# Dense stages with token blocks of 364 columns, three to a group, for 272 columns, four to a group

## What is computed

```python
def _rmsnorm(x, g):
    inv = lax.rsqrt(jnp.mean(jnp.square(x), axis=-1, keepdims=True) + RMS_EPS)
    return (x * inv) * g

proj = _rmsnorm(x, g) @ w                       # 1024 -> 3072: q, k, v of two head groups
...
mixed = jnp.concatenate([_rmsnorm(flat(o_a), g_sb), _rmsnorm(flat(o_b), g_dil)], axis=-1) @ w_out
x = x + mixed                                   # 1024 -> 1024
hdn = jax.nn.relu(_rmsnorm(x, g_mlp) @ w_up)    # 1024 -> 4096
return x + jnp.square(hdn) @ w_down             # 4096 -> 1024
```

## Time and profile before

| | us |
|---|---|
| median of 3 runs (2284.97 to 2289.49) | 2288.51 |
| the profiled execution, its own time | 2293.12 |
| its span, first to last instruction | 2291.3 |
| matmuls of TensorE busy in it | 1918.0 (84%) |
| weight loads of TensorE | 1700.2 (74%) |
| VectorE | 894.1 (39%) |
| ScalarE | 713.6 (31%) |
| GpSimd | 383.2 (17%) |

### The profile page before, as it was taken

The page is one execution under the profiler, slowest core; times in us unless marked ns, Lnnn a source line. Parts: engine busy times, 40 slices in busy tenths (PEclk is TensorE's granted clock), DMA queues, the critical chain, the costliest instruction groups (busy, mean ns, idle before and its releaser), DMA issues. The chain is left out here.

```text
span 2291.3 us, 41063 instructions
## 1 busy us (share of the span) xinstructions
PE 1918.0 (84%) x17210; PEld 1700.2 (74%) x17210; DVE 894.1 (39%) x969; ACT 713.6 (31%) x1064; POOL 383.2 (17%) x173
## 2 busy tenths in 40 slices
PE   4999996477777578777777849799999999999997
PEld 4999994354555456555555539789999999999997
DVE  5201103557566455455455564552222122122223
ACT  4101001456555455445445530221211112121122
POOL 2112101000076500000000021212112121121220
PEclk7999996788898899999999979899999999999999
DMA  4222208401111299999999950143334334333332
GB/s 134 76 86 102 86 39 327 154 19 56 51 42 38 67 294 356 341 332 336 352 341 333 342 196 1 55 147 140 134 113 147 127 110 146 128 128 135 120 109 105
DMA packets 172929, 363.57 MB, mean 159 GB/s; under 512 B 21009, under 2 KB 62610, under 8 KB 171666
## 3 DMA queue, kind: packets, MB, share of 16 engines
q1 hardware_dynamic: 168498, 285.51, 37.7%
q0 software_dynamic: 3904, 75.76, 9.1%
q10 hardware_dynamic: 400, 0.53, 0.1%
HBM read 330.48 MB, written 98.11 MB: 187 GB/s over the span
## 5 line engine op out<-in xcount | busy, mean ns | idle before, releaser
L1195 PEld LDWEIGHTS sa_kt<-ident,sa_k_in 128*128 128x128 f32 x1344 | 154.9, 147 | 153.1 <-DMA sa_k_in<-in_cache_sb_k 76.1
L1195 PE MATMUL sa_kt<-ident,sa_k_in 128*128 128x128 f32 x1344 | 177.3, 288 | 80.9 <-DMA sa_k_in<-in_cache_sb_k 41.0
L393 POOL TENSOR_TENSOR mlp_w_lo<-mlp_raw,mlp_w_hi 128x2048 fp32r<-128x2048 f32 x30 | 138.0, 4601 | 585.3 <-ACT mlp_w_hi L439 585.3
L552 DVE TENSOR_TENSOR xT<-xT,mlp_acc 128x1088 f32<-128x1088 f32 x64 | 82.5, 1289 | 278.7 <-PE mlp_acc L144 278.7
L1376 DVE COPY sa_kT<-sa_kt 128x1024 f32<-128x1024 f32 (+1 forms) x88 | 103.5, 1176 | 222.1 <-PE sa_kt L1195 222.1
L144 PE MATMUL mlp_acc<-n_hi,mlp_w_hi 128*128 128x272 f32 x1024 | 171.8, 290 | 21.0 <-POOL mlp_w_lo L120 16.3
L144 PE MATMUL mlp_acc<-mlp_h_hi,mlp_w_hi 128*128 128x272 f32 x1024 | 170.5, 288 | 4.0 <-DVE mlp_h_lo L548 4.0
L144 PE MATMUL mlp_acc<-n_lo,mlp_w_hi 128*128 128x272 f32 x1024 | 170.9, 289 | 0.0
L144 PE MATMUL mlp_acc<-n_hi,mlp_w_lo 128*128 128x272 f32 x1024 | 170.5, 288 | 0.0
L144 PE MATMUL mlp_acc<-mlp_h_hi,mlp_w_lo 128*128 128x272 f32 x1024 | 169.6, 287 | 0.0
L144 PE MATMUL mlp_acc<-mlp_h_lo,mlp_w_hi 128*128 128x272 f32 x1024 | 169.6, 287 | 0.0
(11 more groups left out here) (158 smaller groups left out, 3329.8 us busy)
## 6 DMA issues: line engine op xcount, KB each, us to landing
sa_k_in<-in_cache_sb_k SPq DMA_DIRECT2D x256, 256.0 KB, 5.6
sa_v_in<-in_cache_sb_v SPq DMA_DIRECT2D x256, 256.0 KB, 5.5
out<-in_cache_win_k POOLq DMA_DIRECT2D x16, 2040.0 KB, 8.9
out<-in_cache_win_v POOLq DMA_DIRECT2D x16, 2040.0 KB, 8.9
sa_k_in<-in_cache_win_k SPq DMA_DIRECT2D x80, 256.0 KB, 7.7
sa_v_in<-in_cache_win_v SPq DMA_DIRECT2D x80, 256.0 KB, 7.2
mlp_raw<-in_w_up SPq DMA_DIRECT2D x16, 1024.0 KB, 12.0
mlp_raw<-in_w_down SPq DMA_DIRECT2D x16, 1024.0 KB, 11.8
```

Of the source, the lines that this page charges most:

```text
L393: pool.tensor_tensor(out=ring.lo[:, n % 2, :], in0=ring.raw[:, n % 2, :], in1=ring.hi[:, n % 2, :].bitcast(F32), op=ALU.subtract).then_inc ...
L552: dve.tensor_tensor(in_banks(xT[:, c, :]), in_banks(xT[:, c, :]), acc[:, c % 2, :, 0:BW], ALU.add).then_inc(added, 1)
L1195: last = pe.transpose(kt_ps[:, c, j * P:(j + 1) * P], k_in[:, i % KS, j, c * P:(c + 1) * P], ident[:, :])
```

## The change

The tokens are cut in three blocks of 364 columns, and each row of tokens in SBUF becomes 1092 columns long (`TP`): the 1088 tokens and four columns of zeros. `acc` takes six banks in place of eight. The zeros are written into `xT` by VectorE at the head of `load_tokens`, and into `o_all_T` by GpSimd at the head of its list in the output projection, where ScalarE waits for them (`padded`). Transfers to and from DRAM keep 1088 columns. The passes of ScalarE and VectorE over whole rows in these stages run over 1092.

```diff
-NB = 4
-BW = T // NB
+NB = 3
+BW = 364
+TP = NB * BW
...
             @block.vector
             def _(dve):
+
+                dve.memset(xT[:, :, T:TP], 0.0).then_inc(padded, 1)
                 out_of_psum(dve, dve.tensor_copy, left_out, 0)
+                dve.wait_ge(padded, 1)
...
-        out = st.enter_context(nc.sbuf_tensor(f"{tag}_out", [P, 2, T], F32))
+        out = st.enter_context(nc.sbuf_tensor(f"{tag}_out", [P, 2, TP], F32))
...
-        root = st.enter_context(nc.sbuf_tensor(f"{tag}_root", [P, groups, T], F32))
+        root = st.enter_context(nc.sbuf_tensor(f"{tag}_root", [P, groups, TP], F32))
...
-                                sp.dma_start(store[ds(row, P), :], out[:, c, :]).then_inc(stored[c], 16)
+                                sp.dma_start(store[ds(row, P), :], out[:, c, 0:T]).then_inc(stored[c], 16)
...
-                        sp.dma_start(src[:, 2 * i:2 * i + 2, :], rows[:, 2 * i:2 * i + 2, :]).then_inc(src_in[i], 16)
+                        sp.dma_start(src[:, 2 * i:2 * i + 2, 0:T], rows[:, 2 * i:2 * i + 2, :]).then_inc(src_in[i], 16)
...
             @block.scalar
             def _(act):
                 spare = 0
+                if load is not None:
+                    act.wait_ge(padded, 1)
...
             @block.gpsimd
             def _(pool):
+                if load is not None:
+                    pool.memset(src[:, :, T:TP], 0.0).then_inc(padded, 1)
                 split_first(pool, ring)
...
-        h_hi = st.enter_context(nc.sbuf_tensor("mlp_h_hi", [P, GC, T], F32R))
-        h_lo = st.enter_context(nc.sbuf_tensor("mlp_h_lo", [P, GC, T], F32R))
+        h_hi = st.enter_context(nc.sbuf_tensor("mlp_h_hi", [P, GC, TP], F32R))
+        h_lo = st.enter_context(nc.sbuf_tensor("mlp_h_lo", [P, GC, TP], F32R))
...
-        xT = sb("xT", [P, KC, T])
+        xT = sb("xT", [P, KC, TP])
...
-            hi = st.enter_context(nc.sbuf_tensor("n1_hi", [P, KC, T], F32R))
-            lo = st.enter_context(nc.sbuf_tensor("n1_lo", [P, KC, T], F32R))
+            hi = st.enter_context(nc.sbuf_tensor("n1_hi", [P, KC, TP], F32R))
+            lo = st.enter_context(nc.sbuf_tensor("n1_lo", [P, KC, TP], F32R))
```

More of the change, by code:

```diff
@@ L70, in load_tokens @@
         turn_done, left_out, right_out = cx.sem("x_turn_done"), cx.sem("x_left_out"), cx.sem("x_right_out")
+        padded = cx.sem("x_padded")
         with nc.Block() as block:
@@ L174, in dense_stage @@
         acc_done, acc_out = cx.sem(f"{tag}_acc_done"), cx.sem(f"{tag}_acc_out")
+        padded = cx.sem(f"{tag}_padded")
         results = [(s, c, g) for s in range(2) for c in range(2) for g in range(groups)]
@@ L348, in mlp_stage @@
         ring = WeightRing(nc, cx, st, "mlp")
-        act_h = st.enter_context(nc.sbuf_tensor("mlp_h", [P, 2, T], F32))
-        h_hi = st.enter_context(nc.sbuf_tensor("mlp_h_hi", [P, GC, T], F32R))
-        h_lo = st.enter_context(nc.sbuf_tensor("mlp_h_lo", [P, GC, T], F32R))
+        act_h = st.enter_context(nc.sbuf_tensor("mlp_h", [P, 2, TP], F32))
+        h_hi = st.enter_context(nc.sbuf_tensor("mlp_h_hi", [P, GC, TP], F32R))
+        h_lo = st.enter_context(nc.sbuf_tensor("mlp_h_lo", [P, GC, TP], F32R))
         acc = st.enter_context(nc.psum_tensor("mlp_acc", [P, 2, NB, 512], F32))
-        root = st.enter_context(nc.sbuf_tensor("mlp_root", [P, T], F32))
+        root = st.enter_context(nc.sbuf_tensor("mlp_root", [P, TP], F32))
         squared, added_up, summed, rooted, inverted, x_hi_done, x_lo_done = (cx.sem(f"mlp_{n}") for n in (
@@ L1516, in decoder_step @@
         with ExitStack() as st:
-            hi = st.enter_context(nc.sbuf_tensor("n2_hi", [P, KC, T], F32R))
-            lo = st.enter_context(nc.sbuf_tensor("n2_lo", [P, KC, T], F32R))
-            with nc.sbuf_tensor("o_all_T", [P, KC, T], F32) as o_in:
+            hi = st.enter_context(nc.sbuf_tensor("n2_hi", [P, KC, TP], F32R))
+            lo = st.enter_context(nc.sbuf_tensor("n2_lo", [P, KC, TP], F32R))
+            with nc.sbuf_tensor("o_all_T", [P, KC, TP], F32) as o_in:
                 dense_stage(nc, cx, "out", a["w_out"][0], o_in, g_out, ones, 2, hi, lo, D_MODEL // 512, load=oT_dram,
```

## The result

The kernel with three blocks of 364 columns took 2313.77 us (median of 4 runs, 2308.34 to 2322.84), the kernel before beside it 2289.0 (4 runs, 2284.97 to 2290.04): 24.8 us more by the medians, and by the means a **ratio of 1.0115, 95% interval 1.0079 to 1.0152**. The forecast was 2265.5 and its range ended at 2297. The profiled execution took 2308.34 us, its span 2306.8, against 2291.3 before: 15.5 us to account for, in what is the fastest of the four runs.

A forecast was written before the change was run, and what follows sets the result against it. TensorE's matmul stream was taken to bound the three dense stages. Terms -15.4 - 8.2 + 0.5 + 0.25 = -23 us took the median from 2288.51 to 2265.5 us, range 2244 to 2297.

The forecast's parts named there:

- The excess of a matmul: In the dense stages each matmul costs a fixed 11.7 ns (MLP) or 12.4 ns (projections) beyond its columns; chance 0.50.
- -15.4 and -8.2 us: Savings claimed from three blocks of 364 for four of 272: 15.4 us in the MLP, 8.2 us in the projections.
- Rival 1: In the dense stages a matmul's excess grows with its columns: -3 to +4 us, 2286 to 2293 us; chance 0.25.
- the low clock: Some 30 matmul groups near the waits, at 1.2 GHz: 303 ns per matmul, nothing won, +0.5 us against the sum.
- the fixed end: The reading of the dense-stage matmul price with a fixed excess: 163.3 ns for 364 columns in the MLP.
- DMA: Transfers: no issue added or moved in its queue, same 1088 columns, rows 16 bytes longer; no cost in the sum.
- Rival 3: Block starts no longer at multiples of 64 bytes cost 6.7 ns per dense-stage matmul: +23 us, 2312 us; chance 0.16.
- Rival 2: Each dense-stage matmul's weight load paces the stream, so 364 columns take 154.7 ns: -83 us, 2206 us; chance 0.09.
- TensorE's waits in the dense stages: Waits keep their lengths: 13.9 us for the first split weights in the projection, 4.0 us in all in the MLP.
- VectorE and ScalarE: Their passes over 1088 columns grow 0.37%, hidden behind TensorE except in the three preparations: +0.25 us.
- the zeros: Memsets on VectorE (128 columns took 0.17 us) and GpSimd (estimated below 0.5 us), both hidden behind existing waits.
- no wait for weights: A weight slot lasts 24, then 23.5 us; refilling takes 1.9 us on ScalarE and 4.6 us on GpSimd.

The follow-up runs named there:

- the last experiment: Changed kernel, moved on by 128 bytes, with varied matmul widths and starts: 364-column groups took 510, 490, 500 ns (aligned to 256 bytes, 16 past, 4 past).

## Why the prediction was wrong, step by step

- **The excess of a matmul** is the step that failed first: "I take the excess as fixed per matmul". At 364 columns it is 166.7 - 151.7 = 15 ns, not 11.7, and at 512 it is 20. The 15 ns is the very point from which, as the prediction worked out, the gain is nothing. So the -15.4 and -8.2 us did not come; the dense stages gave 4.3 us in the one profiled pair and some 3 over all profiles, while kernels with the same places differ by 2.5 us in their medians, which is not told from zero. Rival 1 had this right: 498.8 to 501.8 ns a group and -3 to +4 us, with 500 ns measured in the MLP and some -3 us. One step of the working is off besides: an excess of 14 ns would leave 3 ns a group, not 2, and some -7 us, not -5; nothing hangs on it.
- **What misled** were rows that could not show it: at the low clock, and in plain fp32 with its two periods a column, columns pass at half the pace. The prediction said of the low clock that "a fetch limit would hide there too", and still took the fixed end as the nearer. What holds a column at 0.455 ns rather than 0.417 was not found; that it is a limit of the fetch is argued, not shown. Whether columns or the 16-byte lines of rival 1 are counted, no run can tell, since every width tried is a whole number of lines. The rule of the Trainium skill that the prediction weighed ("TensorE: Matmul & The Clock Gate", section "Back-to-back issue gap", 2.5 ns beside the columns) would put 364 columns at 154.2 ns, an estimate; the trace has 166.7. The section gives that rule for the gap of a single matmul and says that a stream with a weight load for each, as here, goes otherwise, which the prediction left out.
- **DMA** is the term that was missing: "No issue is added and none moves in its queue; stores and loads carry the same 1088 columns". True of the dense stages; but the prediction held that the change "touches these three stages alone", put the rest at nothing, and never asked where the transfers of the other stages land once `xT` is longer. What it left out cost +22 us by the rates, 24 (2308.63 - 2284.72) by the move alone. With the places restored, the changed kernel's 2282.91 us lies inside the range, which would have been luck: the cheaper matmul that the range was built on is not there.
- **Rival 3** named 2312 us, near the result, by another cause: dearer starts. Its mechanism fell twice, by the starts in the last experiment and by the changed kernel with its places restored. A time that fits is no proof of the reason.
- **Rival 2**, the weight load as pace: if the 103 ns at 128 and 192 columns are the load, it lies below the 125 of the kernel before and paces neither kernel.
- **Right:** the low clock (303 ns, as worked out); TensorE's waits in the dense stages, unchanged; VectorE and ScalarE, hidden; the zeros (0.09 us on VectorE and 0.12 us on GpSimd in the trace after, both with nobody waiting); no wait for weights.

No version beat the kernel before: with places at multiples of 256, blocks of 272 and of 364 columns both give its time, within what the medians tell.

## What to carry to other kernels

An array that grows moves every array allocated behind it; before costing a change of size, list the addresses before and after, and look where the transfers of DMA-bound stages land: with cache blocks landing off a multiple of 256 bytes, this one paid 1.1 to 1.4% of the whole time. A price that is read at one width has two readings, per instruction and per column, and rows at another clock or in another mode don't decide between them: one run with several widths does. When a stage that nobody touched gets slower, compare its transfer rate first, and undo the move alone.

## What was not expected of the hardware

- Blocks of 2048 bytes a partition that land 32, 64 or 128 bytes past a multiple of 256 in SBUF pass at 323 to 328 GB/s, at a multiple of 256 at 338 to 345. The packets under 100 ns take 87.2 to 87.4 ns on average for 84.3 to 84.6, however far past they begin.
- A single-pass matmul of split float32 takes some 0.457 ns a column at the full granted clock from 320 to 512 columns, with hardly a fixed part (480 columns between narrow matmuls excepted), yet one period a column at the lower clock, within the view's step (303 ns for 364 at a granted clock of 0.50).
